# Two-layer retention and differential-attention trunk on one core: 64-row score matmuls, loops written out, the keys' power moved ahead, and remainders formed in two instructions a half

## The reference

```python
for l in range(DEPTH):                        # DEPTH = 2
    x += MixerBlock(RMSNorm(x))               # D_MODEL = 1024
    x += ConvGLU(RMSNorm(x))                  # D_FF = 2816, causal conv of width 3
```

## Time and profile before

| | |
|---|---|
| median of 3 runs | 2338.13 us (2333.85 to 2341.69) |
| profiled execution, own time | 2338.67 us |
| its span, first to last instruction | 2336.9 us |
| PE busy | 2289.2 us (98%), 17512 matmul records |
| DVE, ACT, POOL busy | 1135.4, 959.1, 851.4 us |
| mean granted clock of TensorE | 0.990 |

### The profile page before, as it was taken

The page is one execution under the profiler, slowest core; times in us unless marked ns, Lnnn a source line. Parts: engine busy times, 40 slices in busy tenths (PEclk is TensorE's granted clock), DMA queues, the critical chain, the costliest instruction groups (busy, mean ns, idle before and its releaser), DMA issues.

```text
span 2336.9 us, 49860 instructions
## 1 busy us (share of the span) xinstructions
PE 2289.2 (98%) x17512; PEld 2183.4 (93%) x17512; DVE 1135.4 (49%) x1912; ACT 959.1 (41%) x1820; POOL 851.4 (36%) x380
## 2 busy tenths in 40 slices
PE   7999999999999999999999999999999999999999
PEld 6889888999999999999998888899999999999999
DVE  5554464334635575166254644533445466632652
ACT  4545444334423443244245445534343234433442
POOL 4233141323534333433451332322333343344343
PEclk9999999999999999999999999999999999999999
DMA  4232122221222222222322222122122222223213
GB/s 159 65 104 68 59 91 71 78 79 60 75 89 82 83 91 76 98 91 74 100 88 67 80 90 68 64 80 82 63 77 73 88 77 90 86 76 103 91 60 116
DMA packets 81656, 193.53 MB, mean 83 GB/s; under 512 B 7504, under 2 KB 36528, under 8 KB 81456
## 3 DMA queue, kind: packets, MB, share of 16 engines
q1 hardware_dynamic: 59696, 173.50, 22.9%
q10 hardware_dynamic: 21760, 17.45, 2.3%
HBM read 177.50 MB, written 13.42 MB: 82 GB/s over the span
## 4 chain that ended last, share of the span: by engine, by line
PE 71%; issue 19%; POOL 6%; DVE 2%; DMA 0%; ACT 0%; POOLq 0%; DVEq 0%; ACTq 0%
PE ps L615 13%; PE ps L617 13%; PE ps L616 13%; PE ps L1020 4%; PE ps L1021 4%; PE ps L1022 4%; PE ps L657 4%; PE ps L658 4%; PE ps L659 4%; POOL wlo L492 4%; POOL rstd L498 2%; PE ps L892 1%; PE ps L684 1%; PE ps L666 1%; PE ps L665 1%
## 5 line engine op out<-in xcount | busy, mean ns | idle before, releaser
L492 POOL TENSOR_TENSOR wlo<-raw,whi 128x1024 fp32r<-128x1024 f32 (+1 forms) x330 | 759.1, 2322 | 1319.6 <-ACT whi L1078 1319.6
L615 PE MATMUL ps<-hl,whi 128*128 128x272 f32 x2432 | 703.7, 289 | 0.0
L617 PE MATMUL ps<-hl,wlo 128*128 128x272 f32 x2432 | 700.6, 288 | 0.0
L616 PE MATMUL ps<-hl,whi 128*128 128x272 f32 x2432 | 699.1, 287 | 0.0
L615 PEld LDWEIGHTS ps<-hl,whi 128*128 128x128 f32 x2432 | 458.8, 189 | 1.5
L617 PEld LDWEIGHTS ps<-hl,wlo 128*128 128x128 f32 x2432 | 457.3, 188 | 0.0
L616 PEld LDWEIGHTS ps<-hl,whi 128*128 128x128 f32 x2432 | 456.9, 188 | 0.0
L1078 ACT ACTIVATE whi<-raw 128x1024 fp32r<-128x1024 f32 (+1 forms) x330 | 312.9, 996 | 225.1 <-PE ps L1022 176.9
L657 PE MATMUL ps<-whi,hl 128*128 128x256 f32 x1216 | 349.9, 288 | 2.2 <-POOL wlo L492 1.4
L658 PE MATMUL ps<-wlo,hl 128*128 128x256 f32 x1216 | 343.2, 282 | 0.0
L659 PE MATMUL ps<-whi,hl 128*128 128x256 f32 x1216 | 342.8, 282 | 0.0
(11 more groups left out here) (230 smaller groups left out, 3507.0 us busy)
## 6 DMA issues: line engine op xcount, KB each, us to landing
raw<-in_w_units_dram SPq DMA_DIRECT2D x260, 512.0 KB, 4.6
raw<-in_w_down_units_dram SPq DMA_DIRECT2D x64, 352.0 KB, 3.3
out_new_k_prompt_dram<-rawk ACTq DMA_DIRECT2D x8, 512.0 KB, 3.0
out_new_v_prompt_dram<-vd ACTq DMA_DIRECT2D x8, 512.0 KB, 3.0
raw<-in_w_first_dram SPq DMA_DIRECT2D x6, 512.0 KB, 5.0
out_y_dram<-x SPq DMA_DIRECT2D x8, 272.0 KB, 5.9
kc_n<-in_cache_k_dram SPq DMA_DIRECT2D x8, 256.0 KB, 2.9
vc_n<-in_cache_v_dram SPq DMA_DIRECT2D x8, 256.0 KB, 3.3
```

The costliest lines, as they stand in the source:

```text
L492: e.tensor_tensor(wlo[:, s, a:b], raw[:, s, a:b], whi[:, s, a:b].bitcast(F32), ALU.subtract).then_inc(*S.up("w_ready", ("lo", j, part)))
L615: e.matmul(out, wh, hi, start=(c == 0), stop=False)
L616: e.matmul(out, wh, lo, start=False, stop=False)
L617: ins = e.matmul(out, wl, hi, start=False, stop=(c == KC - 1))
```

## The change

It has six parts.

1. Scores: `qz` becomes `qdT` without zeros; the two components' matmuls contract over partitions 0 to 63 and 64 to 127. ACT copies all 128 partitions at once, DVE's four copies (L1724, L1727) go, and two small copies make `qs` for the sample rows.
2. POOL's order in D is lo 1, power q, power k, lo 2, lo 3, lo 4. ACT forms hi 2 after v1 and hi 3 between the evictions of g0 and g1, and squares the queries at the stage's very start. In D's first pass (p = 0) the query transposes come after v2. The banks of the projection tiles are exchanged, with a third one for k2.
3. `lo` forms each half of a unit in two instructions, with one semaphore at the second's end.
4. The loops over layers and D's passes are written out in Python: waits are on constants, and the `settle` instructions and register work go. Each engine's program becomes one straight line.
5. The norm squares and sums of layer 0 come ahead of the lambda work, and those of the next layer at the end of G; they run at the end of the last layer as well.
6. In S, POOL forms both halves of lo S1 and then the row power, and clears the buffers after it.

```diff
-            qz = sb("qz", [P, 2, 2 * TOK], F32, s)
+            qdT = sb("qdT", [P, 2, TOK], F32, s)
+            qs = sb("qs", [P, 2, 2 * DEC], F32, s)
...
+        D_BANKS = dict(k=("mm0", "mm1", "t", "mm0", "o"), v=("mm1", "mm0", "mm1", "mm0", "o"))
...
-                    e.tensor_tensor(wlo[:, s, a:b], raw[:, s, a:b], whi[:, s, a:b].bitcast(F32), ALU.subtract).then_inc(
+                    mid = (a + b) // 2
+                    e.tensor_tensor(wlo[:, s, a:mid], raw[:, s, a:mid], whi[:, s, a:mid].bitcast(F32), ALU.subtract)
+                    e.tensor_tensor(wlo[:, s, mid:b], raw[:, s, mid:b], whi[:, s, mid:b].bitcast(F32), ALU.subtract).then_inc(
                         *S.up("w_ready", ("lo", j, part)))
...
-            with S.layers() as l:
-                with S.body("S"):
-                    for s in ("mm_ready", "act_step", "dve_step", "cs_out"):
+            for l in S.layers():
+                for _ in S.bodies("S"):
+                    lo("S", 1)
+                    norm_power("t")
+                    for s in ("act_step", "dve_step", "cs_out"):
                         e.wait_ge(*S.at(s, k=0))
...
-                    lo("S", 1, (0,))
-                    norm_power("t")
-                    lo("S", 1, (1,))
-                with S.body("D") as p:
+                for p in S.bodies("D"):
                     lo("D", 1)
                     power(20, "q")
+                    power(20, "k")
                     lo("D", 2)
-                    power(20, "k")
                     lo("D", 3)
                     lo("D", 4)
...
-                        if m == 1:
+                        if m == (2 if p == 0 else 1):
                             e.wait_ge(*S.at("tables", k=0))
                             e.wait_ge(*S.at("dve_step", ("rope", "q")))
...
                             for c in range(2):
-                                o = c * (TOK + DEC) + ib * P
-                                ins = e.matmul(pv(bank, P, keys, c * 512), qz[:, hh, o:o + P], kdT[:, hh, 0:keys],
+                                rows = slice(c * DIFF_HD, (c + 1) * DIFF_HD)
+                                ins = e.matmul(pv(bank, P, keys, c * 512), qdT[rows, hh, ib * P:(ib + 1) * P], kdT[rows, hh, 0:keys],
                                                start=True, stop=True)
...
+                    square(rawq, "q")
                     prev = None
...
-                            if u == 0 and m == 0:
-                                square(rawq, "q")
                             if u == 1 and m == 0:
...
                                 square(rawk, "k")
+                            if u == 1 and m == 1:
                                 hi("D", 2, 0)
                                 hi("D", 2, 1)
-                            if u == 1 and m == 2:
+                            if u == 1 and m == (3 if p == 0 else 2):
...
-                                    e.activation(qz[0:DIFF_HD, hh, 0:TOK], pv(f"s{hh}", DIFF_HD, TOK), ACT.Copy,
+                                    e.activation(qdT[:, hh, :], pv(f"s{hh}", P, TOK), ACT.Copy,
                                                  scale=DIFF_HD ** -0.5).then_inc(*S.up(f"act_free_s{hh}", ("q", hh)))
-                    hi("D", 3, 0)
-                    hi("D", 3, 1)
...
                         for kind, tt in filled_at(n):
+                            if (kind, tt) == ("g", 1):
+                                hi("D", 3, 0)
+                                hi("D", 3, 1)
...
                         next_norm(KC - 1, 0)
                         next_norm(KC - 1, 1)
+                        for c, part in CUT:
+                            norm_square(c, part)
...
-                        e.tensor_scalar(qz[DIFF_HD:P, hh, TOK + DEC:TOK + DEC + SEQ], ps[DIFF_HD:P, BANK[f"s{hh}"]:BANK[f"s{hh}"] + SEQ], DIFF_HD ** -0.5, None, ALU.mult).then_inc(
...
+                    e.wait_ge(*S.at("act_free_s1", ("q", 1)))
+                    for c in range(2):
+                        rows = slice(c * DIFF_HD, (c + 1) * DIFF_HD)
+                        e.tensor_copy(qs[rows, :, c * DEC:(c + 1) * DEC], qdT[rows, :, SEQ:TOK]).then_inc(*S.up("dve_step", key=("qs", c)))
...
+                    if phase == "G":
+                        for c, part in CUT:
+                            if c and part != 0:
+                                norm_sum(c, part)
```

More of the change, by code:

```diff
@@ L144, in __init__ @@
         self.phase = "P"
-        self.here, self.waited, self.pending = {}, {}, set()
+        self.here, self.waited = {}, {}
         self.last = None
-    @contextmanager
     def layers(self):
         self.leave()
-        with self.e.Fori(0, DEPTH) as l:
+        for l in range(DEPTH):
             self.layer = l
@@ L154, in layers, with bodies, first @@
         self.layer, self.phase, self.index, self.here, self.waited = None, "end", None, {}, {}
-    @contextmanager
-    def body(self, phase):
+    def bodies(self, phase):
         times = dict(ORDER)[phase]
[L159 to L162, removed]
+        for i in range(times):
+            self.phase, self.here, self.last, self.waited = phase, {}, None, {}
+            self.index = i if times > 1 else None
+            yield i
             self.leave()
[L164 to L168, removed]
+    def first(self):
+        return not self.layer and not self.index
     def leave(self):
-        if self.pending:
-            self.settle()
         self.last = None
+        if not self.first():
+            return
         per = self.seen.per.setdefault(self.phase, {})
@@ L209, in up @@
     def up(self, sem, key=None, n=1):
-        self.pending.clear()
         self.here[sem] = self.here.get(sem, 0) + n
-        if key is not None:
+        if key is not None and self.first():
             assert (self.phase, sem, key) not in self.seen.keys, (self.phase, sem, key)
@@ L220, in note @@
     def note(self, sem, key):
[L222 to L227, removed]
+        if self.first():
+            self.seen.keys[(self.phase, sem, key)] = self.here[sem]
     def prime(self, sem, n):
@@ L550, in pool_program @@
                         lo("M", j)
-                with S.body("F"):
+                for _ in S.bodies("F"):
                     lo("F", 1)
@@ L555, in pool_program @@
                         lo("F", j)
-                with S.body("G"):
+                for _ in S.bodies("G"):
                     for j in range(1, UNITS["G"] + 1):
@@ L667, in n_tile, with n_unit @@
                     ready(ins, ("N", j, m), ("end", j))
-            def n_unit(j, X, XS, dve=False, before=None, after=None, chunk=None, last_bank=None):
+            def n_unit(j, X, XS, dve=False, before=None, after=None, chunk=None, banks=(None,) * TILES):
                 for m in range(TILES):
@@ L692, in pe_program @@
             e.wait_ge(*S.at("pool_step", "one"))
-            with S.layers():
-                with S.body("S"):
+            for _ in S.layers():
+                for _ in S.bodies("S"):
                     start()
@@ L862, in pe_program @@
                     values(9)
-                with S.body("R"):
+                for _ in S.bodies("R"):
                     start()
@@ L931, in pe_program @@
                             *S.up("s_ready", ("snew", hh)))
-                with S.body("M"):
+                for _ in S.bodies("M"):
                     start()
@@ L1143, in act_program @@
             e.activation(aT[:, 0, 0:2 * DEPTH], aT[:, 0, 8:8 + 2 * DEPTH], ACT.Exp).then_inc(*S.up("act_step", key="lexp"))
-            with S.layers() as l:
-                with S.body("S"):
-                    for c, part in CUT:
-                        norm_square(c, part)
+            for l in S.layers():
+                for _ in S.bodies("S"):
                     sample_copies()
@@ L1804, in dve_program @@
                     e.wait_ge(*S.at("s_ready", ("q", 1)))
-                    sample_sum(rawq[0:DEC, NT, :], "mm0", ("N", 3, 4), "q'")
-                with S.body("R"):
+                    sample_sum(rawq[0:DEC, NT, :], "mm1", ("N", 3, 4), "q'")
+                for _ in S.bodies("R"):
                     for hh in range(RET_HEADS):
```

100 lines of the change are left out of this document (35 added, 65 removed).

## The result

The median went from 2338.5 us to 2298.03 us (2297.59 to 2299.23): a ratio of 0.983, 95% interval 0.981 to 0.985, so some 40 us. The forecast was 12 us, with a range of 2309 to 2346 us.

A forecast was written before the change was run, and what follows sets the result against it. PE was taken as the bound, busy 2289.2 of 2336.9 us. Gains of 49.6 us less costs of 37.5 gave net -12.1 from 2338.7: 2326.6 us, as a median 2326, with a range of 2309 to 2346 us.

The forecast's parts named there:

- keys' waits and the clock behind them: D stages: moving the keys' power ahead removes 20.4 us of PE waits and 20 us of low clock, 40.4 us gained.
- layer 0, gained: Start of layer 0: sums ahead of the lambda work remove PE's 2.65 us wait and low clock behind it, 4.35 us.
- layer 0, new waits and clock: Start of layer 0: new waits for lo S1, bank mm0 and lo 2, plus 1.7 us of clock, cost 9.4 us.
- loops, register work: PE's register work and loop edges: writing the loops out gains 2 us, below it 0.
- lo 2 late: D stages: lo 2 comes late for g0, about 1.5 us in six stages (9 us), 2.4 us in layer 1.
- 64-row scores: D-stage scores: sharing one of four slots saves 15.5 us, 64 changes of rows cost 25.6, net +10 us.
- tail: Kernel's end: squares and sums also follow the last norm, unhidden; with the closing barrier +5.2 us.
- Rival (e): Scores: two slots shared between the row halves, -15.5 us, 2310.5 us; chance 0.06.
- (b): Scores: the two row halves don't share a slot, +15.5 us, 2341.5 us; chance 0.20.
- (c): D stages: lo 2 isn't late, DVE's large instructions let two pieces pass, -11.4 us, 2314.5 us; chance 0.12.
- (d): D stages: the clock falls after the new wait too, 20 us in eight stages, 2346 us; chance 0.13.
- (f): Straight programs make PE wait for instructions, or D stages meet a late eviction; some 1 us in 20 stages, 2346; chance 0.07.

The follow-up runs named there:

- e9: Kernel before with unit 3 rounded later (behind g1), POOL's order unchanged: 2300.4 us of span, median 2303.15.
- e10: Kernel before with unit 3 rounded later and the keys' power ahead of lo 2: 2300.5 us of span, median 2302.36.
- e6: Kernel before with its loops over layers and D passes written out, nothing else: 2317.9 us of span, 19.0 us shorter.
- e1: Kernel after, but both components' score matmuls use all 128 rows: 2310.1 us of span, 13.8 us longer than the kernel after.
- e2: Kernel after, but both components' score matmuls use rows 0 to 63: 2329.1 us of span, 32.8 us longer than the kernel after.
- e4: Kernel after without the squares and sums behind the last layer's norm: 2292.0 us of span, 4.3 us shorter than the kernel after.
- e7: Kernel before with the keys' power ahead of unit 2's remainder, nothing else: 2343.6 us of span, 6.7 us longer.
- e3: Kernel after with the keys' power back behind unit 2's remainder: 2324.0 us of span, 27.7 us longer than the kernel after.
- e5: Kernel after with each half of a remainder in one POOL instruction: 2289.5 us of span, 6.8 us shorter than the kernel after.
- e11: Kernel after with one-instruction remainder halves, no last-norm squares and sums, sample-query copies moved ahead of the keys' rotation: 2280.7 us of span, median 2282.82.
- e8: Kernel before with both components' score matmuls on 64 rows, nothing else: 2328.8 us of span, 8.1 us shorter.

## Why the prediction was wrong

I set each term of the sum against what the traces and runs show, in us of span. Where the source is a run against the kernel before, or that kernel's trace, a term is uncertain by some us.

| term | forecast | measured | from |
|---|---|---|---|
| keys' waits and the clock behind them | -40.4 | -36.5 | e9, e10 |
| layer 0, gained | -4.35 | -4.35 | the wait for `acc` and the fall behind it gone |
| layer 0, new waits and clock | +9.4 | +9.5 | waits 1.43, 0.72, 0.94, 1.85, 1.20; 6.8 us at half clock |
| layer 1's start | -2.8 | -2.8 | both waits gone |
| loops, register work | -2 | -7 | below; e6 gives some -6 |
| lo 2 late | +11.4 | +8.5 | six of 0.96; 0.70 and 2.00 in layer 1 |
| 64-row scores | +10 | -12.3 | e1, e2 |
| start of the first matmul | +0.5 | +0.6 | the two traces |
| later exponential | +1 | 0 | the two traces |
| tail | +5.2 | +4.9 | the two traces; 5.2 in e4's |
| sum | -12 | -39.5 | span: -40.6 |

**The step that failed is the 64-row scores:** "I take the middle", one slot shared, net +10. It is mis-sized by 22 of the 28 us that the forecast misses, and has the wrong sign. The other terms miss by 5 us together; that this is so little is partly luck, since the keys' 3.9 and the loops' 5 us have opposite signs. The slot (0.43 us) and the change of rows (0.38 there and back, 0.40 forecast) were read rightly. Wrong was the reason for the middle, that "each half's own two records must follow one another", as if this kept the other half waiting: the records start in pairs, 31.6 us saved instead of 15.5. Also wrong was the number of changes, 64 at full price: 19.4 us instead of 25.6. At 128 columns a share of two slots is also saved (0.21 us a call), which I had ruled out. Rival (e) had this mechanism and 2310.5 us at a chance of 0.06, far too low. The Trainium skill's page TensorE: Matmul & The Clock Gate (Part 3: Packing small matmuls) says that matmuls on different row groups start about 4 ns apart; here it is 7 ns, and it holds for float32, whose matmul is two records.

**The loops** brought 7 us, not 2. Outside the D stages a layer is 1.4 us shorter, half of it the wait of 0.63 us for `acc` in F, which isn't there any more. In the D stages e1, with scores as before, has 79.44 us, 0.96 of it waiting; e10 has 79.00. That is 0.5 us less a stage, about half of it e10's waits for the exponential, the rest work between the matmuls. Twice 1.4 and eight times 0.5 is 7. e6, from the other side, leaves some 6.

**The keys:** their wait and the clock behind it went, as forecast, and no new wait touches the clock in those stages; so the sum was nearly right and rivals (b), (c), (d) and (f) are out. Of the 3.9 us by which e9 stays under the forecast, 2.0 are its eight waits of 0.25 us for the exponential; the rest is within the scatter of the kernel before. But the reason on record was wrong in one point. It gave the gain to the power's place and said of the late unit 3: "nothing". e7 and e9 show the reverse for the kernel before: the order alone costs 5 to 7 us, unit 3's rounding alone gains 32 to 36. In the forecast's own timeline the rotation's 0.36 us each rested on lo 3 being away, and that came from this move. Because the change also rounds unit 2 a tile later, the order is needed there (e3: 27.7 us without it). That the late unit 2 is the reason is read from timelines and not from a run of its own: lo 2 starts 20.8 us after the stage's start in e3 and 19.2 in e9, the power ends at 29.3 and 27.4, and lo 3 begins at 33.4 and 33.6.

**lo 2** was late for the forecast reason, and its pieces ended where they were put: 1.3, 3.8, 6.3 and 7.6 us behind the power's end, forecast 1.25, 3.75, 6.15 and 7.55. The wait is 0.96 us and not 1.5 because the power ended 2.6 us sooner than forecast (the mean took 0.18 us, and the stage began 2.3 us sooner) and PE came 2.1 us sooner. The clock stayed at 1.00 behind 0.96 and 2.00 us. **The remainder in two instructions** is the cause of that wait (e5), which the forecast put down to the order alone. The tail and both starts were right in their sums; single waits of layer 0 were not (lo 2: 3.05 us instead of 4.7, the clock 3.4 instead of 1.7).

What stays open: why the loops' registers cost what they cost inside a D stage, and why the clock fell for 6.8 us in layer 0's first D stage in the kernel after and not at all in e5 and e11. It begins right behind a wait of 1.85 us for lo 2; e5 and e11 have waits of 0.2 and 1.8 us there.

## What to carry to other kernels

When an engine is late, look at who shares its port during every instruction of the chain, not only at what stands in front of it: here the large culprit was the next unit's remainder in the rotation's way, and moving its trigger by a few microseconds was worth 32 to 36 us, while moving the power forward into the same collision cost 5 to 7. Where two float32 matmuls of half the rows can stand side by side on different halves, count half the slots for the pair and about 0.4 us for each change of rows there and back (0.38 here), which long calls earn back and calls of 128 columns don't, and put such calls next to each other, since the change is then paid once. A repair shows the next wait: e5's took away 0.96 us and uncovered 0.74, and only the two together gave the 76.7 us stage.

## What the runs showed of the hardware that was not expected

- Matmuls on rows 0 to 63 and on rows 64 to 127 run side by side record by record (starts 7 ns apart); on the same half they don't (e2).
- The same wait of 2.55 us for the keys was followed by 0, 3.4, 6.8 or 10.2 us at half clock in different stages and kernels (before, e8), and one of 0.64 us by 3.4 us in e8 and by none in before; 2.00 us among dense matmuls by none. The length of a wait alone doesn't tell the fall.
- A small copy on DVE (0.40 us for two) took 4.54 us when POOL was at a remainder (e5), and the mean (0.18 us) 1.74 us in the earlier trace rows. Two large ones in each other's way pay on both sides: in e5 two halves of a remainder took 6.00 us instead of 4.7, and DVE's two instructions of 1.49 us took 3.68 and 3.56.
- The scatter of the times doesn't follow the loops alone: the kernel before goes from 2333.9 to 2341.7 us and the kernel after from 2297.6 to 2299.2, but e10, with its loops as before, only from 2301.6 to 2302.8, and e8, also with them, from 2324.2 to 2337.2. What sets it isn't shown.
